# A transformer block with a PEER layer on one core: low halves of u between decoding steps, earlier v loads, and high halves of u on GpSimd beside the gates

## The reference, cut to what matters

```
q = (x wq) in 8 heads and 2 halves;  s = q . sub_keys            # 128 keys on each side
sv, si = top_k(s, 16);  cand = sv[0] + sv[1];  top, pos = top_k(cand, 16)
eidx = si[0][pos // 16] * 128 + si[1][pos % 16];  g = softmax(top)
a   = gelu(u[eidx] . x);   out = sum over (head, k) of (g * a) * v[eidx]
```

## Time and profile before

| | |
|---|---|
| median of 3 runs | 1582.21 us (1581.47 to 1583.97) |
| profiled execution | 1585.76 us, span 1583.9 us |
| busy: PE, PEld | 1537.8 us (97%), 1352.3 us (85%) |
| busy: DVE, ACT, POOL | 1324.8 us (84%), 652.9 us (41%), 487.0 us (31%) |
| DMA | 398.76 MB, mean 252 GB/s |
| mean granted clock | 0.997 |

### The profile page before, as it was taken

The page is one execution under the profiler, slowest core; times in us unless marked ns, Lnnn a source line. Parts: engine busy times, 40 slices in busy tenths (PEclk is TensorE's granted clock), DMA queues, the critical chain, the costliest instruction groups (busy, mean ns, idle before and its releaser), DMA issues.

```text
span 1583.9 us, 24380 instructions
## 1 busy us (share of the span) xinstructions
PE 1537.8 (97%) x8195; PEld 1352.3 (85%) x8195; DVE 1324.8 (84%) x2859; ACT 652.9 (41%) x1135; POOL 487.0 (31%) x450
## 2 busy tenths in 40 slices
PE   4999999999998999999999999999999999999997
PEld 4888766688998999999989999999999998888886
DVE  6688645439998989989689988899999998999977
ACT  3444543233344666647434333333333332332332
POOL 1121300034450000020246554556656663333000
PEclk9999999999999999999999999999999999999999
DMA  9744420022354564766789999999999999999773
GB/s 367 271 163 146 147 94 27 1 83 91 105 178 147 197 220 171 256 225 244 267 333 389 347 336 354 338 343 372 369 371 375 372 346 355 371 353 352 250 238 107
DMA packets 160466, 398.76 MB, mean 252 GB/s; under 512 B 11753, under 2 KB 75369, under 8 KB 158705
## 3 DMA queue, kind: packets, MB, share of 16 engines
q1 hardware_dynamic: 112992, 227.06, 41.2%
q0 software_dynamic: 36864, 134.23, 22.9%
q10 hardware_dynamic: 10514, 36.30, 5.9%
HBM read 359.27 MB, written 38.27 MB: 251 GB/s over the span
## 4 chain that ended last, share of the span: by engine, by line
PE 81%; DVE 13%; DMA 3%; ACT 2%; issue 1%; DVEq 0%; SPq 0%; ACTq 0%
PE bank_S L871 16%; PE bank_T L871 10%; PE bank_T L849 5%; PE bank_O L820 5%; PE bank_O L822 5%; PE bank_O L821 5%; PE bank_G L871 5%; PE bank_S L820 3%; PE bank_S L821 3%; PE bank_S L822 3%; DMA u_raw<-in_u_t 2%; PE bank_O L617 2%; PE bank_S L584 1%; DVE mod_acc L1816 1%; DVE v_sb L1809 1%; DVE v_sb L1822 1%
## 5 line engine op out<-in xcount | busy, mean ns | idle before, releaser
L1406 ACT ACTIVATE v_hi<-v_raw 128x1024 fp32r<-128x1024 f32 x124 | 131.6, 1062 | 323.1 <-PE bank_G L871 323.1
L1378 ACT ACTIVATE u_hi<-u_raw 128x1024 fp32r<-128x1024 f32 x128 | 135.8, 1061 | 257.0 <-PE bank_O L822 127.4
L1174 POOL COPY stage<-eidx 128x1 uint32<-128x1 uint32 (+1 forms) x128 | 76.6, 598 | 474.2 <-DVE eidx L1933 215.8
L820 PE MATMUL bank_S<-h_hi,u_hi 128*128 128x384 f32 x512 | 180.8, 353 | 6.8 <-DVE u_lo L1908 6.8
L1178 POOL DMA_INDIRECT row<-in_peer_u,stage x128 | 147.3, 1151 | 103.8 <-POOL stage L1174 103.8
L820 PE MATMUL bank_O<-h_hi,u_hi 128*128 128x384 f32 x512 | 172.0, 336 | 1.7 <-DVE u_lo L2033 1.7
L822 PE MATMUL bank_S<-h_hi,u_lo 128*128 128x384 f32 x512 | 172.3, 337 | 0.0
L821 PE MATMUL bank_S<-h_lo,u_hi 128*128 128x384 f32 x512 | 172.3, 336 | 0.0
L822 PE MATMUL bank_O<-h_hi,u_lo 128*128 128x384 f32 x512 | 172.0, 336 | 0.0
L821 PE MATMUL bank_O<-h_lo,u_hi 128*128 128x384 f32 x512 | 171.6, 335 | 0.0
L1997 DVE SCALAR_TENSOR_TENSOR y<-row,wgt,y 128x1024 f32<-128x1024 f32 x128 | 165.9, 1296 | 0.0
(11 more groups left out here) (333 smaller groups left out, 3592.4 us busy)
## 6 DMA issues: line engine op xcount, KB each, us to landing
u_raw<-in_u_t SPq DMA_DIRECT2D x128, 512.0 KB, 4.6
v_raw<-in_peer_v SPq DMA_DIRECT2D x128, 512.0 KB, 6.8
gates<-g_out ACTq DMA_DIRECT2D x12, 2048.0 KB, 7.1
g_in<-gates SPq DMA_DIRECT2D x32, 768.0 KB, 11.0
ada_late<-in_w_ada SPq DMA_DIRECT2D x8, 2048.0 KB, 8.4
spill<-a_act ACTq DMA_DIRECT2D x56, 192.0 KB, 2.1
a_act<-spill SPq DMA_DIRECT2D x14, 768.0 KB, 10.0
w_raw<-in_w_in SPq DMA_DIRECT2D x20, 512.0 KB, 4.0
```

Source lines behind the costliest of these rows:

```text
L820: pe.matmul(ps[:, 0:DT], u_hi[q][:, kk], h_hi[:, GT:NT, k, :], start=(k == 0), stop=False)
L1378: act.activation(u_hi[c % 2][:, :], u_raw[:, c % 2, :], ACT.Copy).then_inc(s_uhi, 1)
L1406: act.activation(v_hi_end[:, i % TAIL, :] if end else v_hi[:, c % 2, :], v_raw[c % 4][:, :], ACT.Copy)\
```

## The change

Five things are altered:

- `BETWEEN` becomes 0 to 23, 32 to 35, 44 to 51, 60 to 63: one chunk more ahead of the first gates, one less behind them.
- VectorE's low halves 19 to 24 are put at other places of `decode_all` and of the first `decode`; the later tiles keep their places, written in another form.
- The high halves n = 2, 3 of each block of gates (chunks 26 to 33, 38 to 45 and 54 to 61) are made by GpSimd's `tensor_copy` instead of ScalarE's activation. They stand ahead of GpSimd's first gathers. ScalarE waits for them before it goes on.
- SP loads v chunks 0 to 3 beside u chunks 59 to 62.
- The high part of v chunk 0 is made inside the last early chunks once the even gate stores are done, and its low part ahead of the main loop; the first round of `chunk` begins with `weigh`.

```diff
-        BETWEEN = [range(0, 23), range(31, 36), range(44, 52), range(60, 64)]
+        BETWEEN = [range(0, 24), range(32, 36), range(44, 52), range(60, 64)]
...
             for i in range(2, EARLY):
                 load_u(i, i)
-            sp.wait_ge(s_idx, NT)
-            for m in range(2):
-                load_v(m, m, False)
+                m = i - (EARLY - 5)
+                if m == 0:
+                    taken(sp, ("cols", NT - GT - 1))
+                if 0 <= m < 4:
+                    load_v(m, m, False)
             load_u(EARLY, 0)
             load_u(NEXT, 1)
...
             sp.wait_ge(s_g[0], 16)
-            load_v(2, 2, False)
             load_u(NEXT + 1, 0)
-            load_v(3, 3, False)
             load_g(1, 1, False)
...
+            def u_high(i):
+                pool.wait_ge(s_uhi, i)
+                pool.wait_ge(s_a, i - 1)
+                pool.wait_ge(s_u[i % 2], 16 * (i // 2 + 1))
+                pool.tensor_copy(u_hi[i % 2][:, :], u_raw[:, i % 2, :]).then_inc(s_uhi, 1)
             for i in range(FIRST_LOW):
                 split_u(i, i)
+            for tb in range(BLOCKS):
+                for n in range(2, 4):
+                    u_high(beside(tb) + n)
             pool.wait_ge(s_idx, NT)
...
                         if b == 3:
-                            u_high(i + 2, i + 2)
                             early_gelu(i)
...
-                    u_high(i + 3, i + 3)
                     early_gelu(i + 1)
+                act.wait_ge(s_uhi, BETWEEN[tile + 1].start + 2)
                 for i in BETWEEN[tile + 1]:
                     u_high(i + 2, i + 2)
                     early_gelu(i)
-            for parity in range(2):
-                act.wait_ge(s_gst[parity], 16 * (BLOCKS // 2))
-            v_high(0, 0)
+                    if i == EARLY - 2:
+                        act.wait_ge(s_gst[0], 16 * (BLOCKS // 2))
+                        v_high(0, 0)
+            act.wait_ge(s_gst[1], 16 * (BLOCKS // 2))
...
                 done(dve, dve.tensor_copy(side16[:, 0, :, :, :].rearrange("p t k h -> p t h k"),
                                           one.rearrange("p (t h k) -> p t h k", t=NT, h=PH)), s_dv)
+                split_u(FIRST_LOW + 2)
...
                                                 ALU.is_equal), s_dv)
+                    for n in chunks[s][0]:
+                        split_u(n)
...
                                                 .to_broadcast([P, TOPK, TOPK, PH]), ALU.mult), s_dv)
-                    for n in chunks[2 * s:2 * s + 1]:
+                    for n in chunks[s][1]:
                         split_u(n)
...
-                    for n in chunks[2 * s + 1:2 * s + 2]:
+                    for n in chunks[s][2]:
                         split_u(n)
...
-                pending = list(BETWEEN[tile])[1:] if tile else list(range(FIRST_LOW + 2, BETWEEN[0].stop))
-                decode(tile + GT, s_idx if tile else s_dv, pending[0:4])
                 if tile == 0:
+                    first, last = FIRST_LOW + 3, BETWEEN[0].stop
+                    decode(GT, s_dv, [([first], [], [first + 1]), ([], [first + 2], [])])
                     normalise()
+                    rest = list(range(first + 3, last))
+                else:
+                    rest = list(BETWEEN[tile])[1:]
+                    decode(tile + GT, s_idx, [([], rest[0:1], rest[1:2]), ([], rest[2:3], rest[3:4])])
+                    rest = rest[4:]
...
             done(dve, dve.memset(y0[:, :], 0.0), s_dv)
             dve.wait_ge(s_gm, DT // 4)
-            for parity in range(2):
-                dve.wait_ge(s_gst[parity], 16 * (BLOCKS // 2))
...
-                if isinstance(i, int) and i == 0:
-                    split_v(i, c)
-                    weigh(i, c, late)
-                else:
-                    weigh(i, c, late)
+                weigh(i, c, late)
+                if not (isinstance(i, int) and i == 0):
                     split_v(i, c)
...
+            dve.wait_ge(s_gst[0], 16 * (BLOCKS // 2))
+            split_v(0, 0)
+            dve.wait_ge(s_gst[1], 16 * (BLOCKS // 2))
             chunk_loop(dve, chunk_and_tile)
```

More of the change, by code:

```diff
@@ L1937, in _ @@
             for tile in range(NT - GT):
-                pending = list(BETWEEN[tile])[1:] if tile else list(range(FIRST_LOW + 2, BETWEEN[0].stop))
-                decode(tile + GT, s_idx if tile else s_dv, pending[0:4])
                 if tile == 0:
+                    first, last = FIRST_LOW + 3, BETWEEN[0].stop
+                    decode(GT, s_dv, [([first], [], [first + 1]), ([], [first + 2], [])])
                     normalise()
+                    rest = list(range(first + 3, last))
[3 more added lines that the diff above has]
+                    rest = rest[4:]
                 if tile == NT - GT - 1:
-                    decode(0, s_idx, pending[4:8])
-                for n in pending[8 if tile == NT - GT - 1 else 4:] + [BETWEEN[tile].stop]:
+                    decode(0, s_idx, [([], rest[0:1], rest[1:2]), ([], rest[2:3], rest[3:4])])
+                    rest = rest[4:]
+                for n in rest + [BETWEEN[tile].stop]:
                     split_u(n)
```

## The result

The changed kernel takes 1592.12 us (median of 6 runs, 1590.36 to 1593.46) against 1582.12 us for the kernel before in the same series. The ratio is 1.0059, 95% interval 1.0046 to 1.0072: slower by 9.3 us, 7.3 to 11.4. The profiled execution took 1592.70 us.

The account below looks back on a forecast made before the run. TensorE, busy 97% of the span, was taken as the bound, with VectorE nearly full beside the gates. 1585.76 + 16.7 + 0.4 - 6.0 - 0.6 - 1.0 = 1595.3, against the median 1591.7 us; range 1574 to 1604.

Parts of the forecast that it names:

- Low halves and the chunk more: Between decoding steps and before the first gates: fewer TensorE waits and less lower clock, gain 6.0 us, bounds 4.5 to 7.2.
- Mechanism beside the gates: Beside gates, VectorE's `hot_i`, `hot_j` and `u_lo` exclude GpSimd's copy, which adds its own length to VectorE's order.
- rival in which `hot_i` lets GpSimd pass: Beside gates, a 1.04 us copy fits under four `hot_i` and costs nothing; 1575 us, chance 0.22.
- starved copy: Beside gates, the copy runs only once VectorE waits for `s_uhi` at its low half; 26 us, 1601 us, chance 0.12.
- Its size, 16.7 us: Three gates stages: 21 copies at 0.84 us, 17.6 us, less 0.9 us because VectorE starts each stage ahead.
- 0.95 us less 0.11 us to spare is 0.84 us: Per chunk beside gates: copy length, middle of 0.86 and 1.04 us, less VectorE's spare time; TensorE stands still 0.84 us.
- My lower bound for the hold, the columns alone at 0.86 us: Beside gates: a 1024-column copy taken by its columns alone from GpSimd's selects, 0.86 us; upper bound 2.40 us.
- v loads and gathers, -1.0 us: Start of main loop: of 1.5 + 1.7 us of waits 1.0 gained; bounds 3.2 gained and 3 lost.
- what spills past 782 is paid back there by the two other v loads: Start of main loop: late gathers push about 3 us of DMA past 782; two moved v loads give back 2.6.
- Between the gates, -0.2 us net: Between gates stages: less cover for decoding costs 0.4 us; high halves not queued on ScalarE gain 0.6 us.
- the share for GpSimd's last copies: Behind gates, two `u_hi` no longer queue behind the last `g_out` and the store's issue: about 0.3 us in each of two stages.
- What would show it: Signs: `hot_j` waits of 15 to 20 us in gates, lengthened VectorE work, stages about 68 us, the 4.67 us wait gone.

Follow-up runs that it names:

- idle runs: Changed kernel with high halves back on ScalarE, GpSimd running an instruction nobody reads at the same 24 places; 128x1024 copy 1594.8 us, rounding to fp32r 1595.3 us.
- half copy: Changed kernel with high halves back on ScalarE, GpSimd making a 128x512 copy nobody reads at the same 24 places; 1587.0 us, ratio 1.0027.

## Why the prediction came out right, point by point

The forecast was 1591.7 us, slower by 9.5; measured was slower by 9.3. The parts agree less well than the sum: that the sum came out within 0.2 us is luck. The gates were put 4.2 us too high and the start of the main loop 3.4 us too low, and these two errors nearly cancel.

- **Low halves and the chunk more, -6.0 us.** Right: -5.7 in the stretch of the profile and -5.7 in the run with this part alone. The waits of 0.4 and 0.45 us that I had put before chunk 20 and the first gates are there as 0.41 and 0.41; the clock stayed up.
- **Mechanism beside the gates.** Right, and shown from both sides: with the copies alone the gates go from 60.3 to 64.4 us, without them they go back, and a copy that nobody reads does the same. The rival in which `hot_i` lets GpSimd pass is refuted, and so is that of a starved copy: a copy begins as soon as the chunk is through, its record is 1.1 us, not lengthened, and it is VectorE that stands. All copies inside the gates met a `hot_i`, so that `hot_j` and `u_lo` exclude a copy as well, which I had also read from the earlier trace rows, is not shown. Why the one-element copy there needed 2.07 us, where a copy of 1024 columns gets in at once, stays open.
- **Its size, 16.7 us, was over-estimated.** The step "0.95 us less 0.11 us to spare is 0.84 us" measured 0.71 less 0.11, 0.60 (burst of 1.82 against 1.11 us); the three stages sum to 12.5 us. The copy itself is 1.10 us by its record, near the 1.04 I took from the selects. What I had wrong is that the copy adds its own length: VectorE works on until the held `hot_i` is due to be over, and loses only the rest. My lower bound for the hold, the columns alone at 0.86 us, was too high for a copy that comes at this moment. Seven copies per stage fit: six at 0.60 us and the first at 0.88 less 0.11, less the 0.3 us of lead that I had estimated, make 3 x (3.60 + 0.47) = 12.2 us.
- **v loads and gathers, -1.0 us, was the wrong sign.** The profile has +2.4. The step that failed is that what spills past 782 is paid back there by the two other v loads. The spill does not queue behind 782 as a mass; it delays the two transfers for which everything waits just then, a load of u (9.1 us) and the gates' load (8.7 us), and then a spell of lower clock follows. Late gathers cost 4.6 us without any copy beside the gates, the v loads give 2.2, and 2.4 is the difference. I had 3 us lost as the bound.
- **Between the gates, -0.2 us net**: -0.4 in the profile, too small to be tested; the share for GpSimd's last copies was not seen.
- **What would show it.** I had asked for 15 to 20 us of waits for `hot_j`. The view has 2.8 us, and 1.9 us for `g_out`. The waits view names only a small part of what the stages lost; the stage lengths, the distance between two copies and the chain are what show it. The idle time of the weight loads shows it as well, 13.3 us more. TensorE's busy row hides it: in 601.7 to 662.7 us it has 61.00 us busy before and 59.76 after, while the matmuls recorded there fell from 441 to 413.

From single parts: -5.7 (low halves) - 2.2 (v loads) + 12.5 (copies) + 4.6 (gathers) = +9.2 us, against +9.3 measured. What the place in the burst does is shown by the changed kernel itself. Open is why the copy comes 0.40 us into the burst there and 0.31 to 0.35 us in the idle runs; the idle code has one semaphore wait less in front of the copy and other operands, and neither was varied.

## What to carry to other kernels

Before work is given to an idle engine, look whether it is idle because it cannot run beside the others: ask for a row where its instruction overlaps one of the busy engine, and multiply by how full that engine is. VectorE had 0.11 us to spare per chunk, so of each copy's 1.10 us 0.60 went into the total. In the idle runs the copy came less than 0.1 us earlier in the burst, and that cost another 0.16 us each time. And when an instruction is put ahead of others on an in-order engine, follow those behind it: three gathers moved by 70 us cost more than a third of what all the copies did.

## What the runs showed of the hardware

- A GpSimd copy of 128x1024 fp32 in SBUF lasts 1.03 to 1.12 us beside `hot_i`, 128x512 0.61 to 0.66, a memset of 128x1024 0.95.
- GpSimd gets in between two scalar operations of VectorE at once and then holds them: one `hot_i` of 128x128 went from 0.34 to 1.05 or 1.22 us. A memset does it too.
- After a copy VectorE goes on when GpSimd's record ends (539.24 us for both). What VectorE loses is less than that record: 0.71 or 0.88 of 1.1 us by where in the burst the copy comes, 0.44 of 0.62 for the half copy, 0.56 of 0.95 for a memset.
- Behind a two-input bf16 product that VectorE had already begun, it is GpSimd that is held: the copy took 1.35 to 1.44 us, while a memset kept its 0.95 us.
